# Second tile's scatter matrices: one wide comparison per step on VectorE, weights multiplied in by GpSimd and ScalarE, four one-hot slots, last expert row on VectorE

## The chip, the cores and the metric

The kernel runs on one core of a Trainium2 chip. The metric is the device time of one execution in microseconds (us). The core has five engines that run side by side, each with an instruction stream of its own, and meet at semaphores: TensorE (PE; PEld is its weight load), VectorE (DVE), ScalarE (ACT), GpSimd (POOL) and SyncE (SP), which here only starts transfers.

## What is computed

Two blocks follow each other on 256 tokens of width 2048. The first (gated MLP and stick-breaking attention) and the mixer of the second are not touched. The change lies in the product-key expert layer at the end, `peer_ffn`:

```python
# per token: 8 heads, 16 picks each = 128 picks out of 128 x 128 experts
s = einsum('thpc,hpnc->thpn', q, keys); sv, si = top_k(s, 16)
cand = sv[:, :, 0, :, None] + sv[:, :, 1, None, :]
cid  = si[:, :, 0, :, None] * 128 + si[:, :, 1, None, :]
top_s, top_j = top_k(cand, 16); eid = take(cid, top_j); gate = softmax(top_s)
act = gelu(einsum('thkd,td->thk', u[eid], x))        # 128 dot products per token
out = einsum('thk,thkd->td', gate * act, v[eid])     # 128 weighted rows per token
```

## The kernel before

The 256 tokens are two tiles of 128, one token per partition. For every pick r (128 a tile, 256 in all) GpSimd gathers one row of `u` per token into a ring of eight slots (line 614), and the dot product with the token's own vector is taken by one of two ways: slots 0, 1, 2, 4, 5 and 6 (`DVE_ROWS`) by a multiply-and-sum on VectorE (line 2076), slots 3 and 7 (`POOL_ROWS`) by a multiplication on GpSimd (line 622) and a sum on ScalarE (line 1323). After the last row of a tile ScalarE applies Gelu to its 128 dot products (line 1336) and VectorE multiplies them by the gates (line 2084): these are the weights.

The first 1440 columns of the output are not gathered. A dense weight matrix w (expert by token) is built and multiplied with all of `v`. Since an expert's number is 128 a + b, the 128 x 128 matrix of one token is the product of two one-hot matrices: `onehot_a` holds, per pick, a one (times the weight) at key a, `onehot_b` a one at key b. That is the scatter. To have picks on partitions, TensorE turns the two keys and the weights of a tile (line 1006, units `picks0` and `picks1`), and ScalarE copies the result to `picksT` (line 1104: row 0 holds a, row 1 b, row 2 the weights). Then there are 32 steps a tile, numbered m, of `SCATTER` = 4 tokens:

- VectorE: one comparison of 4 x 128 elements for `onehot_b` and four instructions of 128 elements that compare and multiply by the weight, for `onehot_a`. Tile 0 (`static_one_hots`, lines 2061 and 2065) is threaded between the dot products of tile 1, one step every three or four rows, and reads the row of numbers 0 to 127 from PSUM (`near_keys`). Tile 1 (`one_hots`, lines 2049 and 2053) stands behind the last dot product, in a hardware loop, and reads the numbers from SBUF (`iota_keys`).
- TensorE: four products into one of two PSUM places (line 1017). It waits for `onehot_done` and for the copy of two steps before (`w_stored`).
- ScalarE: copies the 512 columns to `wT` (line 1350, `store_one`).

There are two one-hot slots, so VectorE waits for the products of two steps before (`scattered`). After the last copy of tile 1 ScalarE rounds the first of `wT` (line 1366) and the stage that multiplies w with `v` begins: TensorE line 1037, with `v` streamed by SyncE (line 526), split by ScalarE (line 1375) and VectorE (line 2168), and the remaining 608 columns gathered by GpSimd (line 644) and added by VectorE (line 2150). The second slot of `v` and all gathers of line 644 but the first two wait until every scatter step is done, since they reuse the one-hot memory. The end of the program is the last layer norm and four stores.

Of the kernel before, what the change touches and what calls it, by code (L numbers as in the profile page):

```python
# [74 lines left out]
SCATTERS = P // SCATTER  # L75

# [11 lines left out]
EXPONENT, FINISH = 5, 8  # L88


def one_hot_row(m):
# [35 lines left out]
       ("picks0", B, False), ("picks1", A, False)]  # L127
# [35 lines left out]
def build(nc, x, norm_g, a_w_in, a_v_norm_g, a_w_s, a_b_s, a_w_out, b_w_in, b_w_out, final_g, ln_in_g_2, ln_in_b_2,  # L163
# [6 lines left out]
    with ctx:  # L170
# [158 lines left out]
        onehot_a = sb("onehot_a", [P, 2, SCATTER, N_KEYS], F32, SCR + 32 * KB)  # L329
        onehot_b = sb("onehot_b", [P, 2, SCATTER, N_KEYS], F32, SCR + 40 * KB)  # L330
# [98 lines left out]
        onehot_done = sem("onehot_done")  # L429
        scattered = sem("scattered")  # L430
# [113 lines left out]
        def _(pool):  # L544
# [82 lines left out]
            for j in range(TILES * BATCHES):  # L627
                s = 0
                for last in POOL_ROWS:
                    scale_row(j, last)  # L630
# [25 lines left out]
        def _(pe):  # L656
# [352 lines left out]
            def scatter(t):  # L1009

                with pe.Fori(0, P // SCATTER // 2) as i:
                    for s in range(2):
                        m = i * 2 + (t * (P // SCATTER) + s)
                        pe.wait_ge(onehot_done, m + 1)
                        pe.wait_ge(w_stored, m + 1)
                        for n in range(SCATTER):
                            last = mm(by_128[B][:, s * SCATTER + n, :], onehot_b[:, s, n, :], onehot_a[:, s, n, :],  # L1017
                                      start=True, stop=True)
                        last.then_inc(scattered, 1)
# [3 lines left out]
            for t in range(TILES):  # L1023
                pe.wait_ge(keys_known, t + 1)
                pe.wait_ge(wgt_done, t + 1)
                turn_picks(f"picks{t}", [pick_keys[:, t, half, :] for half in range(2)]
                           + [wgt[:, t * PICKS:(t + 1) * PICKS]])
                emptied(f"picks{t}")()
                scatter(t)
# [40 lines left out]
        def _(act):  # L1070
# [260 lines left out]
            def pick_gelu(t):  # L1331

                act.wait_ge(rows_used, (t + 1) * BATCHES * len(DVE_ROWS))
                act.wait_ge(rows_summed, (t + 1) * BATCHES * len(POOL_ROWS))
# [19 lines left out]
            def store_w(t):  # L1354

                with act.Fori(0, P // SCATTER // 2) as i:
                    for s in range(2):
                        store_one(t, i * 2 + s, s)
# [19 lines left out]
            for r in range(TILES * PICKS):  # L1378
# [7 lines left out]
                if s in POOL_ROWS:  # L1386
                    sum_row(j, s)
# [6 lines left out]
                for m in range(SCATTERS - 1):  # L1394
                    if r == one_hot_row(m) + 2:
                        store_one(0, m, m % 2)
            pick_gelu(1)
# [27 lines left out]
        def _(dve):  # L1425
# [620 lines left out]
            def one_hots(s, m, token):  # L2046

                dve.wait_ge(scattered, m + 1)
                v.tensor_tensor(onehot_b[:, s, :, :], iota_keys[:, :].unsqueeze(1).to_broadcast([P, SCATTER, N_KEYS]),
                                picksT[:, 1, bass.ds(token, SCATTER)].unsqueeze(2).to_broadcast([P, SCATTER, N_KEYS]),  # L2050
                                ALU.is_equal)
                for n in range(SCATTER):
# [188 lines left out]
```

## Time and profile before

| | us |
|---|---|
| median of 3 runs | 3037.32 |
| lowest and highest run | 3029.28 and 3040.89 |
| the profiled execution, its own time | 3035.28 |
| its span, first to last instruction | 3033.4 |

The profile is of one execution. Its times are counted from the first instruction; 1.9 us of the execution's time lie outside the span. The span has four parts here: dense products up to about 1780, the rows of `u` from there to 2437, the scatter of tile 1 from 2437 to 2495, and the product with `v` from there to 3011, with the last norm behind it. A line of the timeline gives start, duration, engine, line, operation, output and inputs, the count of instructions merged, and in brackets the idle time before it and who ended it.

### The profile page before, as it was taken

The numbers are of one execution on the slowest core, as the hardware profiler recorded it, in microseconds if no ns is written. First come the engines' busy times: TensorE is split into PE (matmuls) and PEld (weight loads), VectorE is DVE, ScalarE is ACT, GpSimd is POOL, SyncE is SP. The second block draws the span as 40 slices with busy tenths as digits, with TensorE's granted clock in tenths as the row PEclk, the third lists the DMA queues.
The fourth block names the chain that finished last, engine by engine and source line by source line (L and its number), as shares of the span: only waits on it lengthen the run. The fifth ranks groups of instructions, "written<-read, shape, count | busy, mean of one in ns | idle before, by whom it ended". The sixth has DMA issues, their size and how long they took to land.

```text
span 3033.4 us, 32464 instructions
## 1 busy us (share of the span) xinstructions
PE 2365.4 (78%) x10883; PEld 1981.4 (65%) x10883; DVE 2103.2 (69%) x2708; ACT 1228.6 (41%) x1293; POOL 830.6 (27%) x614
## 2 busy tenths in 40 slices
PE   8999999999999999899999950000122269999996
PEld 7888888888888888788888740000111158887885
DVE  5456455555444555745665679999998889898998
ACT  5444344444444554343444431212222234444443
POOL 1000000000000000000000048888877815555553
PEclk9999999999999999999999975555555589999998
DMA  8665556555666445555656469999999919999996
GB/s 282 203 185 185 179 179 189 185 193 184 188 187 188 146 163 195 157 169 163 183 185 223 160 254 411 421 417 418 408 411 410 419 49 347 338 346 351 343 344 236
DMA packets 183710, 772.91 MB, mean 255 GB/s; under 512 B 22236, under 2 KB 22288, under 8 KB 149680
## 3 DMA queue, kind: packets, MB, share of 16 engines
q1 hardware_dynamic: 123776, 409.00, 42.6%
q0 software_dynamic: 59824, 362.48, 29.5%
q8 instruction: 65, 1.06, 0.1%
q14 instruction: 45, 0.37, 0.0%
HBM read 769.29 MB, written 2.10 MB: 254 GB/s over the span
## 4 chain that ended last, share of the span: by engine, by line
PE 61%; DVE 19%; issue 8%; DMA 7%; POOL 3%; ACT 2%; DVEq 1%; POOLq 0%; SPq 0%; ACTq 0%
PE half L671 52%; DVE ring L2076 9%; PE half L1037 5%; DMA v_rows<-in_peer_v_rest,eid 3%; DMA ring<-in_peer_u,eid 2%; DMA v_raw<-in_peer_v_dense 2%; PE half L703 2%; POOL v_rows L644 2%; POOL ring L614 1%; DVE v_split L2168 1%; DVE onehot_a L2053 1%; DVE onehot_a L2065 1%; PE half L683 1%; DVE h L2150 1%; DVE v_odd L2150 0%
## 5 line engine op out<-in xcount | busy, mean ns | idle before, releaser
L671 PE MATMUL half<-w_split,xT 128*128 128x512 f32 x7008 | 1610.6, 391 | 8.0 <-DVE xT L1483 5.5
L671 PEld LDWEIGHTS half<-w_split,xT 128*128 128x128 f32 x7008 | 1314.3, 188 | 281.6 <-DVE xT L1483 7.0
L1436 DVE TENSOR_TENSOR w_split<-w_raw,w_split 128x1024 fp32r<-128x1024 f32 x592 | 722.3, 1225 | 740.8 <-ACT w_split L1082 739.8
L1082 ACT ACTIVATE w_split<-w_raw 128x1024 fp32r<-128x1024 f32 x592 | 626.2, 1059 | 910.1 <-PE half L671 875.1
L1037 PE MATMUL half<-v_split,w_x 128*128 128x512 f32 (+1 forms) x2304 | 507.4, 381 | 9.7 <-ACT v_split L1375 5.4
L1037 PEld LDWEIGHTS half<-v_split,w_x 128*128 128x128 f32 x2304 | 431.1, 188 | 85.8 <-issue 11.2
L2076 DVE CUSTOM_DVE_ANT_0 ring<-ring,half 128x2048 f32<-128x2048 f32 x192 | 434.1, 2284 | 47.5 <-DMA ring<-in_peer_u,eid 34.5
L644 POOL DMA_INDIRECT v_rows<-in_peer_v_rest,eid x256 | 280.7, 1097 | 286.6 <-issue 130.4
L1375 ACT ACTIVATE v_split<-v_raw 128x720 fp32r<-128x720 f32 x256 | 206.2, 807 | 273.2 <-DMA v_raw<-in_peer_v_dense 224.7
L614 POOL DMA_INDIRECT ring<-in_peer_u,eid x256 | 243.7, 952 | 259.2 <-DVE eid L2008 173.8
L1017 PE MATMUL half<-onehot_a,onehot_b 128*128 128x128 f32 x512 | 105.5, 371 | 256.9 <-DVE onehot_a L2065 240.3
L622 POOL TENSOR_TENSOR ring<-ring,h 128x2048 f32<-128x2048 f32 x64 | 289.4, 4522 | 41.9 <-DMA ring<-in_peer_u,eid 41.6
L548 POOL DMA_DIRECT2D row_a<-in_final_g x1 | 0.5, 537 | 1067.3 <-DVE ao L1698 1067.3
L1323 ACT ACTIVATE ring<-ring 128x2048 f32<-128x2048 f32 x64 | 122.2, 1910 | 412.1 <-POOL ring L622 412.1
L1017 PEld LDWEIGHTS half<-onehot_a,onehot_b 128*128 128x128 f32 x512 | 90.2, 266 | 272.5 <-DVE onehot_a L2065 249.8
L1006 PE MATMUL half<-ident,pick_keys 128*128 128x128 f32 x4 | 1.3, 434 | 341.1 <-DVE wgt L2084 332.4
L2168 DVE TENSOR_TENSOR v_split<-v_raw,v_split 128x720 fp32r<-128x720 f32 x256 | 230.7, 901 | 2.0 <-ACT v_split L1375 0.5
L1006 PEld LDWEIGHTS half<-ident,pick_keys 128*128 128x128 f32 x4 | 0.6, 204 | 341.6 <-issue 341.6
L2150 DVE SCALAR_TENSOR_TENSOR v_odd<-v_rows,wgt,v_odd 128x608 f32<-128x608 f32 x128 | 109.4, 855 | 36.2 <-DMA v_rows<-in_peer_v_rest,eid 32.6
L2150 DVE SCALAR_TENSOR_TENSOR h<-v_rows,wgt,h 128x608 f32<-128x608 f32 x128 | 108.9, 850 | 12.5 <-DMA v_rows<-in_peer_v_rest,eid 9.8
L548 POOL DMA_DIRECT2D row_a<-in_ln_g x1 | 0.5, 531 | 338.5 <-DVE xT L1483 338.5
L1350 ACT ACTIVATE wT<-half 128x512 f32<-128x512 f32 (+1 forms) x64 | 37.9, 592 | 84.9 <-PE half L1017 84.9
(312 smaller groups left out, 1206.0 us busy)
## 6 DMA issues: line engine op xcount, KB each, us to landing
w_raw<-in_a_w_in SPq DMA_DIRECT2D x192, 512.0 KB, 3.6
v_raw<-in_peer_v_dense SPq DMA_DIRECT2D x256, 360.0 KB
w_raw<-in_b_w_in SPq DMA_DIRECT2D x128, 512.0 KB, 3.5
w_raw<-in_w_in SPq DMA_DIRECT2D x112, 512.0 KB, 3.6
w_raw<-in_a_w_out SPq DMA_DIRECT2D x64, 512.0 KB, 4.3
w_raw<-in_b_w_out SPq DMA_DIRECT2D x32, 512.0 KB, 4.1
w_raw<-in_w_out SPq DMA_DIRECT2D x32, 512.0 KB, 4.8
w_raw<-in_peer_wq SPq DMA_DIRECT2D x32, 512.0 KB, 4.0
```

What stands on the lines that cost most here:

```text
L614: nc.gpsimd.indirect_dma_start(out=ring[:, s, :], out_offset=None, in_=peer_u_2[0], in_offset=bass.IndirectOffsetOnAxis(ap=eid[:, r:r + 1] ...
L622: nc.gpsimd.tensor_tensor(ring[:, s, :], ring[:, s, :], h[:, j // BATCHES, :], ALU.mult)\
L644: nc.gpsimd.indirect_dma_start(out=v_rows[r % V_SLOTS][:, :], out_offset=None, in_=peer_v_rest[0], in_offset=bass.IndirectOffsetOnAxis(ap= ...
L671: last = mm(ps[half][:, 2 * t + n, :], xt[:, xp, kk, tok], w_split[:, s, wp, n * BANK:(n + 1) * BANK], start=(k == 0 and xp == 0 and wp == ...
L1017: last = mm(by_128[B][:, s * SCATTER + n, :], onehot_b[:, s, n, :], onehot_a[:, s, n, :], start=True, stop=True)
L1037: ins = mm(flat[t][:, lo:lo + width], w_x[u][:, xp, 1 - t, s, :], v_split[s][:, vp, lo:lo + width], start=first and xp + vp == 0, stop=las ...
L1082: fn(w_split[:, k % SPLIT_SLOTS, 0, :], w_raw[:, k % RAW_SLOTS, :], ACT.Copy).then_inc(hi_done, 1)
L1375: fn(v_split[s][:, 0, cut], v_raw[s][:, cut], ACT.Copy).then_inc(v_hi, 1)
L1436: v.tensor_tensor(w_split[:, s, 1, :], w_raw[:, k % RAW_SLOTS, :], w_split[:, s, 0, :].bitcast(F32), ALU.subtract).then_inc(split_done, 1)
L2076: v.tensor_tensor_reduce(out=ring[:, s, :], in0=ring[:, s, :], in1=flat[1 - r // PICKS], scale=1.0, scalar=0.0, op0=ALU.mult, op1=ALU.add, ...
L2150: v.scalar_tensor_tensor(out=acc, in0=v_rows[m % V_SLOTS][:, :], scalar=wgt[:, bass.ds(i * BODY + m, 1)], in1=acc, op0=ALU.mult, op1=ALU.a ...
L2168: v.tensor_tensor(v_split[s][:, 1, cut], v_raw[s][:, cut], v_split[s][:, 0, cut].bitcast(F32), ALU.subtract).then_inc(v_lo, 1)
```

## The change

- `HOT_SLOTS` = 4: four one-hot slots, in one tensor `onehots` that holds a and b of a slot side by side. VectorE now waits for the products of four steps before, in both tiles.
- Tile 1's steps on VectorE (`plain_one_hots`) are one comparison of 2 x 4 x 128 elements each, without weights, against `near_keys[1]` in PSUM. The hardware loops over the steps on TensorE, ScalarE and VectorE become straight code.
- The weight is multiplied in afterwards, in place: GpSimd for three of the four tokens (`weigh_one_hots`, 384 elements a step, between its second and third gather of `v`), ScalarE for one (`weigh_one_hot`, `ACT_TOKENS` = 1). TensorE waits for both.
- The two keys of tile 1 are turned apart from the weights, as unit `keys1`, right behind the scatter of tile 0. `picks1` holds the weights alone.
- Row 255, the last one, is a row of VectorE (`by_pool`), not of GpSimd and ScalarE.
- On ScalarE the scaling of h (`weigh_h(1)`, line 1340) and the first rounding of v (`round_v(0, 0)`, line 1375) move from in front of the steps of tile 1 into steps 2 and 4, and the last copy of tile 0 and the copy of `keys1` stand before Gelu.

```diff
+HOT_SLOTS = 4
+ACT_TOKENS = 1
+LAST_ROW = TILES * PICKS - 1
+def by_pool(r):
+    return r % GATHER_SLOTS in POOL_ROWS and r != LAST_ROW
...
-        onehot_a = sb("onehot_a", [P, 2, SCATTER, N_KEYS], F32, SCR + 32 * KB)
-        onehot_b = sb("onehot_b", [P, 2, SCATTER, N_KEYS], F32, SCR + 40 * KB)
+        onehots = sb("onehots", [P, HOT_SLOTS, 2, SCATTER, N_KEYS], F32, SCR + 32 * KB)
+        onehot_a = [onehots[:, s, 0, :, :] for s in range(HOT_SLOTS)]
+        onehot_b = [onehots[:, s, 1, :, :] for s in range(HOT_SLOTS)]
...
+            def weigh_one_hots():
+
+                is_emptied(pool, "picks1")
+                for m in range(SCATTERS, TILES * SCATTERS):
+                    first, end = m * SCATTER + ACT_TOKENS, (m + 1) * SCATTER
+                    cut = onehot_a[m % HOT_SLOTS][:, ACT_TOKENS:, :]
+                    pool.wait_ge(onehot_done, m + 1)
+                    nc.gpsimd.tensor_tensor(
+                        cut, cut, picksT[:, 2, first:end].unsqueeze(2).to_broadcast([P, SCATTER - ACT_TOKENS, N_KEYS]),
+                        ALU.mult).then_inc(weighed_by_pool, 1)
...
                     if r == 2:
+                        weigh_one_hots()
                         pool.wait_ge(scattered, TOKENS // SCATTER + 2)
...
+                for m in range(t * SCATTERS, (t + 1) * SCATTERS):
+                    if t:
+                        pe.wait_ge(weighed_by_pool, m - SCATTERS + 1)
+                        pe.wait_ge(weighed_by_act, m - SCATTERS + 1)
+                    else:
                         pe.wait_ge(onehot_done, m + 1)
+                    pe.wait_ge(w_stored, m + 1)
+                    s = m % HOT_SLOTS
+                    for n in range(SCATTER):
+                        last = mm(by_128[B][:, m % 2 * SCATTER + n, :], onehot_b[s][:, n, :], onehot_a[s][:, n, :],
+                                  start=True, stop=True)
+                    last.then_inc(scattered, 1)
...
+            pe.wait_ge(keys_known, 2)
+            turn_picks("keys1", keys_in[1])
+            pe.wait_ge(wgt_done, 2)
+            turn_picks("picks1", [weights_in[1]])
+            scatter(1)
...
+            def weigh_one_hot(m):
+
+                act.wait_ge(onehot_done, m + 1)
+                for n in range(ACT_TOKENS):
+                    token = m * SCATTER + n
+                    cut = onehot_a[m % HOT_SLOTS][:, n, :]
+                    ins = fn(cut, cut, ACT.Copy, scale=picksT[:, 2, token:token + 1])
+                ins.then_inc(weighed_by_act, 1)
...
             pick_gelu(1)
-            store_one(0, SCATTERS - 1, (SCATTERS - 1) % 2)
-            picks_out("picks1", picksT[:, :, P:], 3)
-            weigh_h(1)
-            round_v(0, 0)
-            store_w(1)
+            picks_out("picks1", picksT[:, 2:3, P:], 1)
+            is_emptied(act, "picks1")
+            for m in range(SCATTERS + 2):
+                if m < SCATTERS:
+                    weigh_one_hot(SCATTERS + m)
+                if m >= 2:
+                    store_one(1, m - 2, m % 2)
+                if m == 2:
+                    weigh_h(1)
+                if m == 4:
+                    round_v(0, 0)
...
+            def plain_one_hots(m):
+
+                wide = [P, 2, SCATTER, N_KEYS]
+                token = m * SCATTER
+                dve.wait_ge(scattered, m - 1)
+                v.tensor_tensor(onehots[:, m % HOT_SLOTS, :, :, :],
+                                near_keys[1].unsqueeze(1).unsqueeze(1).to_broadcast(wide),
+                                picksT[:, 0:2, token:token + SCATTER].unsqueeze(3).to_broadcast(wide), ALU.is_equal)\
+                    .then_inc(onehot_done, 1)
...
             weights(1)
-            weights_turned(1)
+            is_emptied(dve, "keys1")
...
-            with dve.Fori(0, P // SCATTER // 2) as i:
-                for s in range(2):
-                    one_hots(s, i * 2 + (P // SCATTER + s), i * (2 * SCATTER) + (P + s * SCATTER))
+            for m in range(SCATTERS, TILES * SCATTERS):
+                plain_one_hots(m)
```

## Rows read from the trace of the kernel before

**Rows 1.** The page, parts 1 and 4: busy time; chain that ended last.

```profile
PE 2365.4 (78%) x10883; PEld 1981.4 (65%) x10883; DVE 2103.2 (69%) x2708; ACT 1228.6 (41%) x1293; POOL 830.6 (27%) x614
...
PE 61%; DVE 19%; issue 8%; DMA 7%; POOL 3%; ACT 2%; DVEq 1%; POOLq 0%; SPq 0%; ACTq 0%
```

**Rows 2.** Busy time by stretch: five engines, granted clock, DMA share, GB/s.

```profile
2300.00:2400.00 100.00, 22.82 (x88) 19.58 (x88) 84.77 (x114) 25.46 (x31) 82.96 (x50) 0.50 1.01 414
...
2441.00:2447.00 6.00, 5.40 (x23) 5.11 (x24) 5.33 (x17) 1.35 (x3) 0.00 (x0) 0.50 0.01 3
2447.00:2453.00 6.00, 4.03 (x31) 3.46 (x30) 5.53 (x18) 2.39 (x4) 0.00 (x0) 0.99 0.00 0
2453.00:2494.00 41.00, 29.28 (x206) 24.51 (x205) 40.16 (x125) 14.94 (x25) 0.00 (x0) 1.00 0.00 0
...
2600.00:2700.00 100.00, 99.71 (x458) 85.33 (x457) 91.76 (x115) 48.30 (x65) 55.50 (x52) 1.00 0.97 349
```

**Rows 3.** Timeline from the last rows of `u` to tile 1's first steps.

```profile
2426.93 2.07 PE L1017 MATMUL half<-onehot_a,onehot_b 128*128 128x128 f32 x8 [7.88 <-DVE onehot_a L2065]
...
2429.00 2.28 DVE L2076 CUSTOM_DVE_ANT_0 ring<-ring,half 128x2048 f32<-128x2048 f32 x1
2430.41 4.50 POOL L622 TENSOR_TENSOR ring<-ring,h 128x2048 f32<-128x2048 f32 x1 [5.40 <-DMA ring<-in_peer_u,eid]
2431.20 0.08 DVE L2076 DVE_READ_ACCUMULATOR2_ANT wgt<- 128x1 f32 x1
2434.94 1.91 ACT L1323 ACTIVATE ring<-ring 128x2048 f32<-128x2048 f32 x1 [6.38 <-POOL ring L622]
...
2437.03 0.31 ACT L1336 ACTIVATE wgt<-wgt 128x128 f32<-128x128 f32 x1
...
2437.38 0.29 DVE L2084 TENSOR_TENSOR wgt<-wgt,gate 128x128 f32<-128x128 f32 x1 [6.09 <-ACT wgt L1336]
...
2438.22 0.42 PE L1006 MATMUL half<-ident,wgt 128*128 128x128 f32 x1
2438.68 0.49 ACT L1104 ACTIVATE picksT<-half 128x384 f32<-128x384 f32 x1 [0.85 <-PE half L1006]
2439.07 0.70 ACT L1340 ACTIVATE h<-h 128x608 f32<-128x608 f32 x1
2439.59 0.69 DVE L2049 TENSOR_TENSOR onehot_b<-iota_keys,picksT 128x512 f32<-128x512 f32 x1 [1.93 <-ACT picksT L1104]
2439.67 1.49 ACT L1375 ACTIVATE v_split<-v_raw 128x720 fp32r<-128x720 f32 x2
...
2441.37 3.79 PE L1017 MATMUL half<-onehot_a,onehot_b 128*128 128x128 f32 x16 [2.72 <-DVE onehot_a L2053]
```

**Rows 4.** Timeline of the last steps of tile 1 and what follows.

```profile
2491.44 0.69 DVE L2049 TENSOR_TENSOR onehot_b<-iota_keys,picksT 128x512 f32<-128x512 f32 x1
...
2492.04 1.11 DVE L2053 TENSOR_SCALAR onehot_a<-iota_keys,picksT 128x128 f32<-128x128 f32 x4
...
2493.21 1.16 PE L1017 MATMUL half<-onehot_a,onehot_b 128*128 128x128 f32 x8 [0.47 <-DVE onehot_a L2053]
...
2494.51 0.60 ACT L1350 ACTIVATE wT<-half 128x512 f32 x1 [1.03 <-PE half L1017]
2495.14 0.63 ACT L1366 ACTIVATE w_x<-wT 128x512 fp32r<-128x512 f32 x1
```

**Rows 5.** Timeline of VectorE at 1754: 1024 elements, and what comes behind.

```profile
1754.09 1.22 DVE L1436 TENSOR_TENSOR w_split<-w_raw,w_split 128x1024 fp32r<-128x1024 f32 x1
1755.23 0.86 DVE L1950 MAX8 sv<-left 128x8 f32<-128x128 f32 x4
```

**Rows 6.** GpSimd's groups: shapes, count, busy us, mean ns, idle before.

```profile
L622 POOL TENSOR_TENSOR ring<-ring,h 128x2048 f32<-128x2048 f32 x64 | 289.4, 4522 | 41.9 <-DMA ring<-in_peer_u,eid 41.6
...
L558 POOL MEMSET ones<- 128x256 f32 x1 | 0.3, 312 | 0.1
...
L554 POOL MEMSET onward<- 128x128 f32 x1 | 0.2, 205 | 0.1
```

**Rows 7.** Line 2061, VectorE beside GpSimd: duration ns min/median/max, starts.

```profile
L2061 DVE TENSOR_TENSOR onehot_b<-half,picksT x32: 685/686/693, 2129.9 to 2425.2; 128x512 f32<-128x512 f32 x32
```

**Rows 8.** Timeline at 2054: a VectorE instruction with both inputs in SBUF.

```profile
2053.51 4.50 POOL L622 TENSOR_TENSOR ring<-ring,h 128x2048 f32<-128x2048 f32 x1 [1.48 <-DMA ring<-in_peer_u,eid]
...
2054.16 4.39 DVE L1979 TENSOR_TENSOR cand<-sv 128x512 f32<-128x512 f32 x1
```

More of the change, by code:

```diff
@@ L88 @@
 EXPONENT, FINISH = 5, 8
+LAST_ROW = TILES * PICKS - 1
+def by_pool(r):
+    return r % GATHER_SLOTS in POOL_ROWS and r != LAST_ROW
+DOTS = sum(not by_pool(r) for r in range(TILES * PICKS))
+SUMS = TILES * PICKS - DOTS
 def one_hot_row(m):
@@ L629, in _ @@
                 for last in POOL_ROWS:
-                    scale_row(j, last)
+                    if by_pool(j * GATHER_SLOTS + last):
+                        scale_row(j, last)
                     while s <= last:
@@ L1009, in scatter @@
             def scatter(t):
-                with pe.Fori(0, P // SCATTER // 2) as i:
-                    for s in range(2):
-                        m = i * 2 + (t * (P // SCATTER) + s)
-                        pe.wait_ge(onehot_done, m + 1)
[L1015 to L1019, printed above, removed]
+                for m in range(t * SCATTERS, (t + 1) * SCATTERS):
[3 more added lines that the diff above has]
+                    else:
+                        pe.wait_ge(onehot_done, m + 1)
+                    pe.wait_ge(w_stored, m + 1)
[4 more added lines that the diff above has]
+                    last.then_inc(scattered, 1)
             pe.sem_inc(scattered, 2)
             emptied("peer_q1")()
[L1023 to L1029, printed above, removed]
+            keys_in = [[pick_keys[:, t, half, :] for half in range(2)] for t in range(TILES)]
+            weights_in = [wgt[:, t * PICKS:(t + 1) * PICKS] for t in range(TILES)]
+            pe.wait_ge(keys_known, 1)
+            pe.wait_ge(wgt_done, 1)
+            turn_picks("picks0", keys_in[0] + [weights_in[0]])
+            emptied("picks0")()
+            scatter(0)
+            pe.wait_ge(keys_known, 2)
[3 more added lines that the diff above has]
+            scatter(1)
             def multiply_v(p, u, s, first=False, last=False):
@@ L1352, in store_one @@
                     .then_inc(w_stored, 1)
[L1354 to L1358, printed above, removed]
+            def weigh_one_hot(m):
[5 more added lines that the diff above has]
+                ins.then_inc(weighed_by_act, 1)
             act.sem_inc(w_stored, 2)
@@ L1393, in _ @@
                     fn(flat[A], h[:, 1, :], ACT.Copy).then_inc(h_copied, 1)
-                for m in range(SCATTERS - 1):
+                for m in range(SCATTERS):
                     if r == one_hot_row(m) + 2:
                         store_one(0, m, m % 2)
+                if r == one_hot_row(SCATTERS - 1) + 2:
+                    picks_out("keys1", picksT[:, 0:2, P:], 2)
             pick_gelu(1)
-            store_one(0, SCATTERS - 1, (SCATTERS - 1) % 2)
-            picks_out("picks1", picksT[:, :, P:], 3)
-            weigh_h(1)
-            round_v(0, 0)
-            store_w(1)
+            picks_out("picks1", picksT[:, 2:3, P:], 1)
[9 more added lines that the diff above has]
+                    round_v(0, 0)
             act.wait_ge(w_stored, TOKENS // SCATTER + 2)
@@ L2044, in bring_near @@
                 halving_by(near_half[t])
[L2046 to L2052, printed above, removed]
-                    ins = v.tensor_scalar(onehot_a[:, s, n, :], iota_keys[:, :], picksT[:, 0, bass.ds(token + n, 1)],
-                                          picksT[:, 2, bass.ds(token + n, 1)], ALU.is_equal, ALU.mult)
-                ins.then_inc(onehot_done, 1)
             def static_one_hots(m):
-                s, token = m % 2, m * SCATTER
-                dve.wait_ge(scattered, m + 1)
-                v.tensor_tensor(onehot_b[:, s, :, :], near_keys[1].unsqueeze(1).to_broadcast([P, SCATTER, N_KEYS]),
+                s, token = m % HOT_SLOTS, m * SCATTER
+                if m > 1:
+                    dve.wait_ge(scattered, m - 1)
+                v.tensor_tensor(onehot_b[s], near_keys[1].unsqueeze(1).to_broadcast([P, SCATTER, N_KEYS]),
                                 picksT[:, 1, token:token + SCATTER].unsqueeze(2).to_broadcast([P, SCATTER, N_KEYS]),
@@ L2064, in static_one_hots @@
                 for n in range(token, token + SCATTER):
-                    ins = v.scalar_tensor_tensor(out=onehot_a[:, s, n - token, :], in0=near_keys[1],
+                    ins = v.scalar_tensor_tensor(out=onehot_a[s][:, n - token, :], in0=near_keys[1],
                                                  scalar=picksT[:, 0, n:n + 1],
```

14 lines of the change are left out of this document (8 added, 6 removed).

## The prediction

> **What bounds the kernel now.** I read from the whole to the place. The page's busy shares and its chain name TensorE first and VectorE second [rows 1], but they average over stages. The table by stretch separates them [rows 2]. In the rows of `u` the transfers are full (DMA share 1.01 at 414 GB/s); in the product with `v` TensorE is busy 99.71 of 100 us. Between the two lies the scatter of tile 1, where transfers and GpSimd stand still and VectorE is busy 40.16 of 41.00 us, TensorE 29.28. So there VectorE sets the pace. The timeline of its last steps [rows 4] shows how: a comparison starts at 2491.44, the four instructions behind it at 2492.04, the next would start at 2493.07 (the products follow at 2493.21): 1.63 us a step, of which 0.60 is the comparison and 1.03 the other four. TensorE's products take 1.16, ScalarE's copy 0.60. The last product ends at 2493.21 + 1.16 = 2494.37, and the product with `v` hangs on it, by the copy at 2494.51 and the rounding at 2495.14. So whatever that end moves, everything behind moves too: behind it stands the same work, and no transfer of it but two pieces of v and two gathers runs ahead. The timeline of the hand-over [rows 3] gives the other piece: VectorE's last dot product ends at 2431.28, and then it waits 6.09 us, for row 255 on GpSimd (2430.41, 4.50 us) and ScalarE (2434.94, 1.91 us), before it may form the weights. The first comparison starts at 2439.59, the first product at 2441.37.
>
> **The change, part by part.**
>
> *Row 255 on VectorE.* It landed by 2430.41 (GpSimd was waiting for its transfer) and VectorE is free for it at 2431.2. The rows' dot product takes 2.28, 2.2 from start to start (2429.00 to 2431.20): done at 2433.5. Gelu then starts at 2433.6 in place of 2437.03, a gain of 3.4. Its cover is row 254: GpSimd's two first gathers of `v` are now issued some 10 us earlier, and 2 x 128 rows x 608 x 4 B = 0.62 MB would take 1.5 us at 414 GB/s if they went before row 255; 0.8 of that lies beside row 254, so 0.7 is the bound. They are issued after it, so I take 0.
>
> *Hand-over.* Gelu 0.31, the weights' multiplication 0.29, with the gap of 0.04 between: done at 2434.3. VectorE needs only the keys now; these were turned behind tile 0's scatter, whose products end at 2429.00, and copied before Gelu, which has 4 us of room. So the first wide comparison starts at 2434.3, not 2439.59. In parallel TensorE turns the weights (0.42 and a reaction, 2434.8) and ScalarE copies 128 columns (about the 0.31 of Gelu's 128): weights there at 2435.3, before the first comparison ends.
>
> *The wide comparison.* 1024 elements: the subtraction of that size takes 1.22, and the instruction behind it starts 1.14 after it [rows 5]; the 512 of now take 0.69 and 0.60, so both fit 0.53 us per 512 plus 0.07. I take 1.13 a step, against 1.63. The operand from PSUM costs nothing: 686 ns from PSUM [rows 7], 0.69 from SBUF.
>
> *GpSimd's multiplication,* 384 elements. Its multiplication of 2048 takes 4.52, and a memset takes 205 ns for 128 and 312 for 256 [rows 6], so about 0.1 is fixed: 0.1 + 384 x (4.42 / 2048) = 0.93, and 0.08 between two instructions: 1.01 a step. Low end: 384/2048 of 4.52 = 0.85. High end: 0.3 fixed (the whole of a small instruction's time) and 0.3 in between, 1.43 a step. I take 1.01, since the operation is the same and in place as well; no row shows its operand repeated along 128 elements. It lies beside VectorE's next comparison, and costs only its latency as long as it is under 1.13. GpSimd's queue has behind it only the gathers from the third on, and those waited for the whole scatter before as well.
>
> The GPSIMD Engine Reference of the Trainium skill, section Engine selection, speaks against this move: elementwise work on two inputs belongs on VectorE, GpSimd being about twice as slow. The rows agree (4.52 against 2.28 for 2048). It would count if GpSimd set the pace; by the 0.93 above it does not, so the sum stays as it is.
>
> *ScalarE:* one weighing (0.31) and one copy (0.60) a step, 0.91 in 1.13, and once 0.70 and 1.49 for the two moved jobs [rows 3]. Before, these two lay beside the first comparisons; now they are in the steps.
>
> *TensorE:* 1.16 for a step alone at the high clock [rows 4]. At the low clock 2.07 alone, and 3.79 for two steps back to back, so 1.71 for a further one [rows 3]; half of it, 0.86, at the high clock. The PSUM places bring 1.16 + 0.14 + 0.60 + 0.07 over two steps: 0.99 a step. Both are under 1.13 once the clock is up.
>
> **The sum.** First product: 2434.3 + 1.22 + 0.08 + 0.93 + 0.07 = 2436.6. The clock was granted at 0.50 until 2447 and in full from there, 5.6 us after the first product [rows 2, 3]; I take the same delay, 2442.3. By then TensorE starts four steps, at 2.07 and then 1.71 to 1.8 each, and the fourth ends at about 2444.0. ScalarE adds its 0.70 and 1.49 there, by which the weighing of the sixth step is done only at 2444.8 and its copy clears the way at 2445.4; its product ends at 2446.6. VectorE runs four steps ahead and is then held: the tenth comparison may start at 2446.7, where at its own pace it would at 2434.3 + 9 x 1.13 = 2444.5. So the start costs 2.2. From there 22 more at 1.13, and the last lasts 1.22: 2446.7 + 24.9 + 1.2 = 2472.8; weighing and reaction 1.0, products 0.07 + 1.16: 2475.0. The end of the scatter moves from 2494.4 to 2475.0, by 19.4: 5.3 from the earlier first comparison, 16 from 32 shorter steps, less 2.2 of start and less some 0.9 for the step's longer path at the end (wider comparison and weighing in series). The profiled execution took 3035.28, so 3015.9; the median of the runs lies 2.04 above it: 3037.3 - 19.4 = 3018.
>
> Costed at nothing: four slots in tile 0's scatter (VectorE waited nowhere for them that mattered; the transfers bound that stage [rows 2]); straight code for the loops (TensorE's streams elsewhere are straight and 99.71% busy); if the fetching of code did cost, it would by a few us, inside the range. The largest gain: no cost at the start, 21.6. The smallest of the forecast's kind: GpSimd at 1.43 a step, 2435.6 + 32 x 1.43 + 1.2 = 2482.6, a gain of 11.8.
>
> **The rivals.**
> - *GpSimd sets the pace.* For: its price is extrapolated, and a margin of 0.12 a step is thin. Against: fixed costs in rows 6 are small. At 1.4 a step the end is at 2481.6 and the time 3037.3 - 12.8 = 3025. At 1.80 a step nothing would be left.
> - *The clock stays low,* since TensorE has short products with waits between them. All 32 steps at 1.71: 2436.6 + 32 x 1.71 + 0.4 = 2491.7, a gain of 2.7, 3035. Against: with gaps of 0.47 in 1.63 us it rose before and stayed at 1.00 [rows 2, 4]; now they are shorter.
> - *VectorE and GpSimd shut each other out, and it gets slower.* Place: each wide comparison against each multiplication. That this exists is in the trace: an instruction of 512 elements with both inputs in SBUF took 4.39 us, not 0.69, and ended as GpSimd's multiplication did [rows 8]. A step would be 1.13 + 0.93 + 0.1 = 2.16, the end at 2434.3 + 32 x 2.16 + 1.2 = 2504.6, 10.2 later: 3047. It decides from 1.80 a step. Against: line 2061, with one input in PSUM as here, took 685 to 693 ns in all 32 instances beside a GpSimd 83% busy [rows 2, 7]. SBUF — State Buffer of the Trainium skill, section Who interferes with whom, says a VectorE instruction with at most one SBUF input doesn't contend with GpSimd; by that rule this rival falls, and the trace agrees with it (693 ns at most).
> - *The last row's move doesn't bring its 3.4,* if the transfer lands later. This costs at most that: 3021.
>
> **How the numbers follow.** The forecast with its neighbours, a gain of 15 to 22, gets 0.75 (the late row included); GpSimd's pace 0.15; the clock 0.05; the lock 0.05. The predicted time is 3018. The range reaches from the largest gain less the scatter of the runs, 3037.3 - 21.6 - 7 = 3009, to GpSimd at 1.43 with some of that scatter, 3037.3 - 11.8 + 3 = 3028. The bound of 0.5% is 15.2 us, about what a measurement of this kernel can tell from no change. The forecast lies 4 us beyond it, and the runs before differ by 11.6 among themselves, so 0.85 of its 0.75 count as faster and a third of GpSimd's case: 0.69. Slower by more than 0.5% needs 2.3 us a step: 0.03. The rest, 0.28, is within.
>
> **What would show it.** The first wide comparison at about 2434, taking 1.22 and followed by the next after 1.13 (right) or held by TensorE throughout (wrong). GpSimd's multiplication near 0.93 and waiting for VectorE each time; if VectorE waits for products and GpSimd is without gaps, the rival holds. Gelu about 0.1 behind row 255 on VectorE. The granted clock at 1.00 from 5 to 6 us after the first product. The last product near 2475, and the product with `v` as long as before (2495 to 3011). If that stage is longer, the gain was given back there, which I do not expect, since none of its inputs arrives otherwise than before.

## The result, and the profile after

The changed kernel takes 3017.51 us (median of 6 runs, 3014.29 to 3022.77) against 3038.43 for the kernel before (6 runs, 3029.28 to 3040.89): 20.9 us less, a ratio of 0.9938 with a 95% interval of 0.9926 to 0.9950. The forecast was 3018, with a range of 3009 to 3028. The profiled execution of after took 3014.29, its span is 3012.6. That the time lies within 0.5 us of the forecast is in part luck: the gain came out 1.5 larger than the 19.4 of the sum, and the kernel before 1.1 above the 3037.3 from which it was taken.

The hand-over and the first steps, in the timeline of the changed kernel (start, duration, engine, line, operation; in brackets the idle time before and who ended it), to be held against [rows 3]:

```profile
2429.50 2.28 DVE L2123 CUSTOM_DVE_ANT_0 ring<-ring,half 128x2048 f32<-128x2048 f32 x1
...
2431.71 2.28 DVE L2123 CUSTOM_DVE_ANT_0 ring<-ring,half 128x2048 f32<-128x2048 f32 x1
...
2434.03 0.31 ACT L1372 ACTIVATE wgt<-wgt 128x128 f32<-128x128 f32 x1 [2.10 <-DVE wgt L2123]
2434.37 0.29 DVE L2131 TENSOR_TENSOR wgt<-wgt,gate 128x128 f32<-128x128 f32 x1 [0.38 <-ACT wgt L1372]
2434.70 5.75 DVE L2113 TENSOR_TENSOR onehots<-half,picksT 128x1024 f32<-128x1024 f32 x5
...
2436.02 0.40 ACT L1396 ACTIVATE onehots<-onehots,picksT 128x128 f32<-128x128 f32 x1 [0.51 <-DVE onehots L2113]
2436.07 0.83 POOL L659 TENSOR_TENSOR onehots<-onehots,picksT 128x384 f32<-128x384 f32 x1 [8.17 <-DVE onehots L2113]
...
2440.77 4.62 DVE L2113 TENSOR_TENSOR onehots<-half,picksT 128x1024 f32<-128x1024 f32 x4 [0.33 <-PE half L1048]
...
2442.23 1.49 ACT L1414 ACTIVATE v_split<-v_raw 128x720 fp32r<-128x720 f32 x2
...
2444.63 7.64 PE L1048 MATMUL half<-onehots 128*128 128x128 f32 x61 [1.03 <-ACT wT L1386]
...
2445.80 6.88 DVE L2113 TENSOR_TENSOR onehots<-half,picksT 128x1024 f32<-128x1024 f32 x6 [0.41 <-PE half L1048]
```

Row 255 follows row 254 on VectorE (2431.71), the first wide comparison stands at 2434.70, and TensorE's first product came at 2436.95. VectorE is held by TensorE twice, for 0.33 and 0.41 us, and never again. (Held means that it waits for the products that free a slot.) Its comparisons then run without a gap, as VectorE's timeline shows when it is taken by itself:

```profile
2445.80 26.11 DVE L2113 TENSOR_TENSOR onehots<-half,picksT 128x1024 f32<-128x1024 f32 x23 [0.41 <-PE half L1048]
```

That is 23 comparisons in 26.11 us. One lasts 1.21 and the next starts 1.13 after it, so a comparison's last 0.08 lies beside the next one, and a hold costs its idle time and these 0.08. The last steps, to be held against [rows 4]:

```profile
2471.94 0.40 ACT L1396 ACTIVATE onehots<-onehots,picksT 128x128 f32<-128x128 f32 x1 [0.24 <-DVE onehots L2113]
2471.99 0.83 POOL L659 TENSOR_TENSOR onehots<-onehots,picksT 128x384 f32<-128x384 f32 x1 [0.30 <-DVE onehots L2113]
...
2472.94 0.97 PEld L1048 LDWEIGHTS half<-onehots 128*128 128x128 f32 x8 [0.16 <-POOL onehots L659]
...
2474.14 0.60 ACT L1386 ACTIVATE wT<-half 128x512 f32<-128x512 f32 x1 [0.53 <-PE half L1048]
2474.77 0.63 ACT L1405 ACTIVATE w_x<-wT 128x512 fp32r<-128x512 f32 x1
```

GpSimd waits 0.30 us a step for VectorE, TensorE 0.16 for GpSimd. By stretch (columns as in [rows 2]):

```profile
2453.00:2470.00 17.00, 16.97 (x123) 14.55 (x122) 17.00 (x16) 13.32 (x32) 12.45 (x16) 1.00 0.01 1
...
2580.00:2680.00 100.00, 100.00 (x461) 86.00 (x460) 92.47 (x117) 47.82 (x65) 56.84 (x52) 1.00 0.98 346
```

In the scatter TensorE is busy 16.97 of 17 us where it was 29.28 of 41, and ScalarE and GpSimd three quarters of the time, but VectorE still without a gap: it is still what sets the pace. TensorE's full share does not speak against it: its weight load waits 0.16 us a step for GpSimd, and behind 2445.80 VectorE is never held by it.

To compare traces I use one interval, which leaves out how long the rest took: from the start of row 254's dot product on VectorE to the first rounding of `wT` (L1366 before, L1405 after). It is 2495.14 - 2429.00 = 66.1 us before and 2474.77 - 2429.50 = 45.3 after, 20.9 less. In front of it the two traces differ by 0.5 us, behind it by as much the other way (538.3 and 537.8 to the end). So the whole gain lies in it, and nothing was given back.

### The profile page after: what moved, and what is told of

Read it like the earlier page. It is cut to its first block, busy times and chain, and to the rows that moved or that the text cites. A ratio compares the mean times of both kernels' runs of the same rounds, so it can differ in the third digit from the quotient of the medians.

```text
span 3012.6 us, 31949 instructions
## 1 busy us (share of the span) xinstructions
PE 2363.1 (78%) x10883; PEld 1980.9 (66%) x10883; DVE 2090.2 (69%) x2582; ACT 1236.3 (41%) x1324; POOL 849.3 (28%) x645
## 3 DMA queue, kind: packets, MB, share of 16 engines
q8 instruction: 69, 1.13, 0.2%
## 4 chain that ended last, share of the span: by engine, by line
PE 64%; DVE 18%; DMA 9%; issue 5%; POOL 2%; ACT 2%; DVEq 0%; SPq 0%; POOLq 0%; ACTq 0%
PE half L699 52%; DVE ring L2123 10%; PE half L1073 6%; DMA v_rows<-in_peer_v_rest,eid 4%; DMA v_raw<-in_peer_v_dense 2%; DMA ring<-in_peer_u,eid 2%; PE half L731 1%; POOL ring L629 1%; PE half L1048 1%; DVE v_split L2215 1%; DVE onehots L2102 1%; POOL v_rows L672 1%; PE half L711 1%; DVE v_odd L2197 0%; PE half L779 0%
## 5 line engine op out<-in xcount | busy, mean ns | idle before, releaser
L1048 PE MATMUL half<-onehots 128*128 128x128 f32 x512 | 102.5, 367 | 241.3 <-DVE onehots L2102 229.0
L1048 PEld LDWEIGHTS half<-onehots 128*128 128x128 f32 x512 | 89.4, 264 | 254.6 <-DVE onehots L2102 238.1
L1386 ACT ACTIVATE wT<-half 128x512 f32<-128x512 f32 x64 | 37.5, 586 | 53.9 <-PE half L1048 53.7
```

The lines of the kernel that those rows point to most:

```text
L1048: last = mm(by_128[B][:, m % 2 * SCATTER + n, :], onehot_b[s][:, n, :], onehot_a[s][:, n, :], start=True, stop=True)
```

## The experiments

Each edit is on the changed kernel unless it says otherwise. The interval, the first comparison and the holds of VectorE by TensorE come from the one trace of each run.

| run | interval | against after | first comparison behind row 254's start | time, us |
|---|---|---|---|---|
| before | 66.1 | +20.9 | 10.59 | 3038.43 |
| after | 45.3 | | 5.20 | 3017.51 |
| old_step | 60.2 | +15.0 | 6.09 | 3031.0 |
| two_slots | 64.2 | +18.9 | 5.21 | 3034.76 |
| three_slots | 47.2 | +2.0 | 5.20 | 3019.86 (one run) |
| keys_from_sbuf | 64.0 | +18.7 | 5.20 | 3036.76 |
| last_row_pool | 49.5 | +4.2 | 8.70 | 3017.76 (one run) |
| before_last_row | 62.3 | +17.0 | 7.09 | 3031.66 (one run) |
| keys_late | 47.2 | +2.0 | 6.44 | 3017.78 (one run) |
| jobs_early | 45.3 | +0.1 | 5.20 | 3016.4 (one run) |
| pool_four | 46.0 | +0.7 | 5.20 | 3017.45 (one run) |
| act_two | 45.7 | +0.5 | 5.20 | 3014.84 (one run) |
| prefill_two | 44.3 | -1.0 | 5.20 | 3016.04 |
| seven_eighths | 51.7 | +6.5 | 5.20 | 3020.98 |

A single time says little here, since the six of after spread over 8.5 us, and the kernel before, measured again beside these runs, had medians of 3037.53, 3034.96 (one run) and 3037.2; I read the interval first. The ratios below are to the kernel before as measured beside the run.

**old_step: what the step's own length carries.** All of the change but the wide step and its helpers.

```diff
-                plain_one_hots(m)
+                static_one_hots(m)        # one comparison of 512, four of 128 with the weight
...
-                        weigh_one_hots()
...
-                if m < SCATTERS:
-                    weigh_one_hot(SCATTERS + m)
```

> The changed kernel, but tile 1's steps on VectorE are the five narrow instructions of before, with the weight (reading the numbers from PSUM); GpSimd and ScalarE multiply nothing in; four slots, straight code, the early keys and row 255 on VectorE stay. My theory, that the length of VectorE's own step carries the gain: 1.63 us a step again, first comparison at about 2435.7 (it must wait for the weights now), last product ends near 2435.7 + 32 x 1.63 + 1.3 = 2489, 15 us later than in the changed kernel; time about 3032.5. Rival, that slots and straight code carry the gain by freeing VectorE of waits: the end stays within 5 us of 2474 and the time under 3023.

Ratio to before 0.9976 (0.9966 to 0.9986); 13.5 us slower than after, and 15.0 in the interval, as the theory had it. Two steps from its timeline of TensorE:

```profile
2472.36 1.16 PE L1043 MATMUL half<-onehots 128*128 128x128 f32 x8 [0.47 <-DVE onehots L2095]
2473.99 1.16 PE L1043 MATMUL half<-onehots 128*128 128x128 f32 x8 [0.47 <-DVE onehots L2095]
```

1.63 us a step again, with TensorE waiting 0.47 for VectorE, as in [rows 4]. VectorE was never held. So of the 20.9, 15.0 hang on the wide step with its helpers. Three pieces make them up: 14.5 between the first comparison and the last (2434.71 to 2485.24 here, 2434.70 to 2470.70 in after), 0.9 because the wide comparison does not wait for the weights (6.09 against 5.20), less 0.4 for the longer path behind the last comparison (3.61 here, 4.07 in after). The other 5.9 are hand-over, slots and straight code: 4.5 of these by the earlier first comparison (6.09 in place of 10.59), the other 1.4 between the first comparison and the last (51.85 in the kernel before, 50.53 here). There VectorE was held twice in the kernel before, for 0.67 and 0.47:

```profile
2443.61 0.69 DVE L2049 TENSOR_TENSOR onehot_b<-iota_keys,picksT 128x512 f32<-128x512 f32 x1 [0.67 <-PE half L1017]
...
2447.50 0.69 DVE L2049 TENSOR_TENSOR onehot_b<-iota_keys,picksT 128x512 f32<-128x512 f32 x1 [0.47 <-PE half L1017]
```

**two_slots and three_slots: whether the slots matter once weighing is a stage of its own.**

```diff
-HOT_SLOTS = 4
+HOT_SLOTS = 2                            # three_slots: 3
-                dve.wait_ge(scattered, m - 1)
+                dve.wait_ge(scattered, m + 1)   # three_slots: m
```

> The changed kernel with two one-hot slots in place of four. With weighing as a stage of its own between VectorE and TensorE, a slot is taken for 1.21 (comparison) + 0.07 + 0.83 (GpSimd) + 0.1 + 1.16 (products) + 0.1 = 3.4 to 3.5 us. Theory: with two slots a step then costs half of that, 1.7 to 1.75, the scatter ends 18 to 20 us later and the whole gain is gone: 3036 to 3038. Rival, that VectorE's 1.13 sets the pace whatever the slots: 3018.

> The changed kernel with three one-hot slots. A slot is taken for about 3.4 us, so three slots allow 1.13 to 1.17 a step, just what VectorE takes. Theory: within 1.5 us of four slots at the full clock, and more holding at the low clock (up to 3 us), so the scatter ends 1 to 4 us later. Rival, that the fourth slot is needed as much as the second pair: 6 us or more.

With two slots the ratio to before is 0.9998 (0.9986 to 1.0011): no gain can be told from the times, and of the interval's 20.9 us 2.0 are left, though each engine does exactly the same work. Its timeline shows VectorE in pairs, waiting for the products between them:

```profile
2469.40 2.52 DVE L2112 TENSOR_TENSOR onehots<-half,picksT 128x1024 f32<-128x1024 f32 x2 [0.94 <-PE half L1048]
...
2472.86 2.52 DVE L2112 TENSOR_TENSOR onehots<-half,picksT 128x1024 f32<-128x1024 f32 x2 [0.94 <-PE half L1048]
```

3.46 us for two steps, 1.73 each, as worked out. Not all of that is GpSimd's: the product waits for two ends that come together, GpSimd's multiplication (2471.53 in the trace) and ScalarE's copy of two steps before, which stands behind its weighing (2471.55). Three slots cost 2.0 us, within the 1 to 4 of the theory; VectorE is held three times there, by 0.88, 0.28 and 0.94, in the first ten steps. Behind them it shows no idle time, but its step is 1.15 (24 comparisons in 27.68 us) and not 1.13, and a third of 3.46 is 1.15: with three slots the slot still sets the pace by a hair, with four (0.87) it does not.

**keys_from_sbuf: the price of the lock that the place in PSUM avoids.**

```diff
-                                near_keys[1].unsqueeze(1).unsqueeze(1).to_broadcast(wide),
+                                iota_keys[:, :].unsqueeze(1).unsqueeze(1).to_broadcast(wide),
```

> The changed kernel, but the wide comparison reads the numbers 0 to 127 from SBUF (iota_keys) in place of PSUM (near_keys), so that it has two SBUF inputs while GpSimd multiplies. Theory (the third rival of the prediction, which the place in PSUM avoids): the two shut each other out, each step is 1.13 + 0.83 + about 0.1 = 2.06 to 2.2, and the scatter ends 29 to 34 us later, 3046 to 3052. Rival: no exclusion between these two operations, 3018.

The mechanism is there. The groups of VectorE and GpSimd in the stretch of the scatter (count, busy us, mean ns, idle before):

```profile
L659 POOL TENSOR_TENSOR onehots<-onehots,picksT 128x384 f32<-128x384 f32 x32 | 55.4, 1767 | 8.2 <-DVE onehots L2113 8.2
L2113 DVE TENSOR_TENSOR onehots<-iota_keys,picksT 128x1024 f32<-128x1024 f32 x32 | 55.3, 1804 | 0.0
```

The same two instructions took 0.827 and 1.210 us each in the changed kernel; here both last about 1.8, one waiting in the other's time, and no idle time shows it. It is not that reading SBUF is slower by itself: the first comparison, with no multiplication beside it yet, took 1.22 us, and the last multiplication, with no comparison beside it any more, 0.82. But its size was wrong, 18.7 in place of 29 to 34. Eight multiplications took 14.16 us, 1.77 a step, while 0.83 + 1.13 = 1.96: so some 0.2 of the two do overlap. What part of them that is, the runs leave open. The time is that of the kernel before, ratio 0.9998 (0.9988 to 1.0007); the interval is 2.2 shorter. This is also the other half of what the Trainium skill's SBUF — State Buffer states in the section Who interferes with whom, that a VectorE instruction with two SBUF inputs contends with a GpSimd instruction that reads SBUF; this run agrees, with 1.80 us for 1.21 on VectorE and 1.77 for 0.83 on GpSimd.

**last_row_pool and before_last_row: the last row undone, and alone.**

```diff
-LAST_ROW = TILES * PICKS - 1
+LAST_ROW = -1
```

and on the kernel before:

```diff
-                    scale_row(j, last)
+                    if j * GATHER_SLOTS + last != LAST_ROW:
+                        scale_row(j, last)
...
-                if s in DVE_ROWS:
+                if s in DVE_ROWS or r == LAST_ROW:
                     dve.wait_ge(row_landed[s], 16 * j + 16)
```

> The changed kernel with row 255 back on GpSimd and ScalarE. Theory: Gelu starts 3.0 us later (2437.0 in place of 2434.0, counted from the landing of row 255) and everything behind it with it: time up by 3. Rival, that a later start is taken up because VectorE has its comparisons ready in four slots: GpSimd then starts with four steps in hand and up to 3 x 0.13 a step is won back, time up by 1 or less.

> The kernel before with this part of the change alone: row 255 goes to VectorE. Theory: Gelu starts 3.5 us earlier against row 254, and since tile 1's steps begin only after the weights, the end of the scatter comes 3.5 us earlier too (66.1 us after the start of row 254 becomes 62.6, as putting it back cost 3.5 in the changed kernel's first comparison). Rival: the clock's time to rise varies by up to 2 us and hides part of it.

Undone, the first comparison comes 3.50 us later (8.70 for 5.20), and the end 4.2; alone on the kernel before, the first comparison comes 3.50 earlier and the end 3.9. So the row is worth 3.5. What is beyond that are holds of VectorE, 0.7 more of them in last_row_pool than in after (below) and one fewer in before_last_row than in the kernel before (0.67 alone). My rival for last_row_pool could not have come true: VectorE starts its comparisons behind the weights in either case, so it had none in hand.

**keys_late: the keys turned with the weights, as before.**

```diff
-            turn_picks("keys1", keys_in[1])
             pe.wait_ge(wgt_done, 2)
+            turn_picks("keys1", keys_in[1])
```

(and ScalarE's copy of them behind Gelu).

> The changed kernel, but the keys of tile 1 are turned and copied only after the weights are known, in front of the weights' own turn, as before the change. Theory: the first comparison comes 1.1 to 1.3 us later (turn of two 0.64, copy 0.38, reactions) and, as VectorE sets the pace, the end too. Rival: GpSimd and TensorE wait for the weights anyway, so nothing moves (under 0.3).

First comparison 1.24 later, as expected, the end 2.0 later.

**jobs_early: ScalarE's two jobs out of the steps.**

```diff
+                if r == LAST_ROW - 3:
+                    round_v(0, 0)
...
                     picks_out("keys1", picksT[:, 0:2, P:], 2)
+                    weigh_h(1)
...
-                if m == 2:
-                    weigh_h(1)
-                if m == 4:
-                    round_v(0, 0)
```

> The changed kernel, but ScalarE's scaling of h and first rounding of v are done while it waits for the last rows of u, not in steps 2 and 4. In the changed kernel TensorE stands for 1.03 us behind the rounding, and VectorE is held twice, 0.33 and 0.41. Theory: without them VectorE is held by 0.3 at most (the low clock's part), the scatter ends 0.4 to 0.7 earlier. Rival: it is all the low clock, no change.

The interval did not move (45.34 for 45.27; 0.4 to 0.7 less was expected), and read alone this says that the jobs cost nothing. But the clock differed. The granted clock rose 3.8 us behind the first product in after, and 5.5 to 5.9 behind it in jobs_early, keys_late and last_row_pool. The holds of VectorE, from the timelines:

| | clock up after | held |
|---|---|---|
| after | 3.8 | 0.33 + 0.41 = 0.74 |
| keys_late | 5.9 | 0.32 + 0.48 + 0.55 = 1.35 |
| last_row_pool | 5.5 | 0.32 + 0.48 + 0.58 = 1.38 |
| jobs_early | 5.7 | 0.32 + 0.48 = 0.80 |

Among the three with the late clock, the jobs account for the third hold, 0.55 to 0.58 us. The late clock costs 0.6 of holds with the jobs in place (1.35 to 1.38 against 0.74), and with the 0.08 of the third hold 0.7, which is just by how much the ends of keys_late and last_row_pool moved more than their starts. I take the jobs' 0.6 as supported, not shown: it rests on three single traces, and why the clock rose when it did stays open.

**pool_four and act_two: how near the helpers are to setting the pace.**

```diff
-ACT_TOKENS = 1
+ACT_TOKENS = 0                           # act_two: 2
```

> The changed kernel with GpSimd weighing all four tokens of a step (512 elements) and ScalarE none. It measures how near GpSimd is to setting the pace. In the changed kernel the multiplication takes 0.827 and stands 0.30 behind the one before. If those 0.30 are a wait for VectorE (my theory), GpSimd needs 4/3 x 0.83 = 1.10 and 0.08 between: 1.18 a step, the scatter ends 1 to 2 us later than in the changed kernel. If they are GpSimd's own gap (rival), a step is 1.40 and the scatter ends 7 to 8 us later.

> The changed kernel with ScalarE weighing two tokens a step and GpSimd two. ScalarE then has 2 x 0.31 to 0.40 and a copy of 0.58, 1.2 to 1.38 a step, over VectorE's 1.13. Theory: ScalarE sets the pace, the scatter ends 3 to 8 us later, GpSimd waits. Rival: its instructions overlap so far that it still keeps up, no change.

pool_four ended 0.7 later, less than the 1 to 2 expected: the multiplication of 512 takes 1.041, not 1.10, and fits into 1.13, with VectorE without a gap from 2446.60 on. The 0.30 were a wait. Of the 0.7 only 0.2 is the longer multiplication; VectorE was held three times at the start (0.48, 0.38 and 0.29, the clock rising 5.1 us behind the first product), which is 0.5 more than in after. In act_two the theory fell: two weighings, a copy, and the step stays at 1.13.

```profile
2463.35 0.69 ACT L1396 ACTIVATE onehots<-onehots,picksT 128x128 f32<-128x128 f32 x2
2463.39 0.61 POOL L659 TENSOR_TENSOR onehots<-onehots,picksT 128x256 f32<-128x256 f32 x1 [0.52 <-DVE onehots L2113]
...
2463.95 0.57 ACT L1386 ACTIVATE wT<-half 128x512 f32<-128x512 f32 x1
...
2464.48 0.69 ACT L1396 ACTIVATE onehots<-onehots,picksT 128x128 f32<-128x128 f32 x2
```

Two weighings of 0.40 each take 0.69 together, and the copy starts 0.60 behind the first: ScalarE's instructions overlap by some 0.1 each, so that durations summed (0.40 + 0.40 + 0.57 = 1.37) overstate what it needs. It shows no idle time in these steps, though, so it has hardly any room left. Of the 0.5 by which the interval is longer, 0.3 lie behind the last comparison.

**prefill_two: two comparisons in VectorE's idle time ahead of the last rows.**

```diff
+KEYS_AT = 26
+PREFILL = {SCATTERS: 247, SCATTERS + 1: 251}     # step: behind which row
...
+                for m, row in PREFILL.items():
+                    if r == row:
+                        is_emptied(dve, "keys1")
+                        plain_one_hots(m)
```

(TensorE turns the keys in front of step 26 of tile 0, and `jobs_early` is in it.)

> The changed kernel plus: tile 1's keys are turned behind step 25 of tile 0, VectorE does the comparisons of steps 32 and 33 while it waits for rows 248 and 252 (idle 1.60 us each there), and ScalarE's two jobs are early as in jobs_early. Theory: GpSimd can start as soon as the weights are there, the first product comes 0.5 to 0.9 us earlier, and VectorE has two comparisons fewer behind the weights; but TensorE at the low clock then holds it, so 1 to 2 us are gained: 3016. Rival, that VectorE's pace alone decides: the full 2.3 us, 3015.

Ratio to before 0.9932 (0.9917 to 0.9947), interval 1.0 us shorter than after's; the first product 6.97 behind row 254's start, not 7.45. The two comparisons cost nothing where they stand, but most of their 2.3 is lost again:

```profile
2413.96 1.22 DVE L2116 TENSOR_TENSOR onehots<-half,picksT 128x1024 f32<-128x1024 f32 x1
2415.65 2.29 DVE L2126 CUSTOM_DVE_ANT_0 ring<-ring,half 128x2048 f32<-128x2048 f32 x1 [0.47 <-DMA ring<-in_peer_u,eid]
...
2436.85 2.35 DVE L2116 TENSOR_TENSOR onehots<-half,picksT 128x1024 f32<-128x1024 f32 x2
2440.74 1.22 DVE L2116 TENSOR_TENSOR onehots<-half,picksT 128x1024 f32<-128x1024 f32 x1 [1.53 <-PE half L1053]
```

With its slots full, VectorE waits 1.53 and then 0.48 for TensorE. So of the theory the lower end came out. It is the best version here by its trace, but 3016.04 against 3017.51 is not a difference that these runs can tell.

**seven_eighths: VectorE's comparison an eighth shorter.**

```diff
+                    nc.gpsimd.tensor_scalar(onehot_a[m % HOT_SLOTS][:, 0, :], iota_keys[:, :],
+                                            keys_by_step[:, m - SCATTERS, 0:1],
+                                            picksT[:, 2, token:token + 1], ALU.is_equal, ALU.mult)
...
-                wide = [P, 2, SCATTER, N_KEYS]
+                wide = [P, 2 * SCATTER - 1, N_KEYS]
```

> The changed kernel plus: GpSimd builds one of the four onehot_a of a step by itself (comparison and weight in one instruction of 128 elements, from SBUF), so VectorE's comparison has 896 elements in place of 1024 (keys stored step by step for it), ScalarE weighs one token, GpSimd two; ScalarE's two jobs are early. If VectorE's own length sets the pace (theory), a step falls from 1.13 to 1.00 and the scatter ends 3 to 4 us earlier, 3014. GpSimd needs about 0.35 + 0.61 + 0.05 = 1.0 for it and could hold it at 1.05. Rival: the two PSUM places and ScalarE's copies already limit a step to 1.13, no gain.

It failed: 6.5 us more in the interval than after, 3020.98, ratio to before 0.9953 (0.9937 to 0.9969). GpSimd's groups in a stretch of the scatter, and VectorE's timeline:

```profile
L661 POOL TENSOR_SCALAR onehots<-iota_keys,keys_by_step,picksT 128x128 f32<-128x128 f32 x23 | 18.1, 788 | 0.0
L664 POOL TENSOR_TENSOR onehots<-onehots,picksT 128x256 f32<-128x256 f32 x23 | 14.0, 609 | 0.0
```

```profile
2459.56 1.09 DVE L2119 TENSOR_TENSOR onehots<-half,keys_by_step 128x896 f32<-128x896 f32 x1 [0.26 <-PE half L1053]
2460.92 1.09 DVE L2119 TENSOR_TENSOR onehots<-half,keys_by_step 128x896 f32<-128x896 f32 x1 [0.26 <-PE half L1053]
```

I had put the small instruction at 0.35, from its neighbours of 0.29 in the profile before; it took 0.788. Both GpSimd groups show no idle time, the step is 1.35 (2459.56 to 2460.92), and VectorE's 0.26 are put down to TensorE only because TensorE comes last in the row: the weight loads wait for GpSimd, so VectorE does too. That is the prediction's first rival in life: at 1.35 a step the interval is 6.5 longer, and 14.4 of its 20.9 remain. Whether 1.00 a step could be had otherwise stays open.

## Why the prediction was right

*What bounds.* Right. VectorE's length of a step set the pace and still does: old_step, which undoes the wide step and its helpers alone, gives back 15.0 of 20.9, and 14.5 of these lie between the first comparison and the last.

*Row 255 and the hand-over.* Right. First comparison at 5.3 behind row 254's start in the sum (2434.3), at 5.20 in the trace. The last row measured 3.5 both ways (predicted 3.4), the early keys 1.24. That the two gathers of `v` ahead of it cost nothing held: no idle time stands in front of row 255.

*The comparison.* 1.13 a step, as taken from [rows 5]; the duration was 1.21.

*GpSimd's multiplication.* On the safe side: 0.93 was taken, with a low end of 0.85, and it took 0.827. The three lengths that the runs have, 0.609, 0.827 and 1.041 for 256, 384 and 512 elements, make 1.69 ns an element and 0.18 fixed, against 2.2 ns an element in [rows 6]. So the fixed part had been put too low and the price of an element too high. That the operand repeated along the elements is what makes an element cheaper is likely, but no run here has a full operand at these lengths.

*ScalarE.* Sized 0.31 a weighing, measured 0.40; without effect, since its instructions overlap.

*The cost of the start* is the term that was mis-sized: 2.2 in the sum, 0.9 in the trace. The tenth comparison starts at 2445.80 where its own pace would bring it at 2434.70 + 9 x 1.13 = 2444.9; that is the 0.74 of holds and twice 0.08. The clock rose 3.8 us behind the first product, not the 5.6 of the kernel before, and by the other traces that is worth 0.7. The other 0.6 lie with ScalarE. Counted from row 254's start, the weighing of the sixth step, behind the rounding of `v`, was done at 14.5 (2444.0) and not at 15.8 as I had it; in last_row_pool, with the late clock, it was done at 15.25 once the 3.5 of the last row are taken off. With these 1.3 too much, 0.1 for the first comparison and 0.1 for GpSimd's shorter multiplication the difference between the predicted gain (19.4) and the measured (20.9) is accounted for.

*The split of the sum.* The times of the sum give 19.4, but the four terms named behind them, 5.3 + 16 - 2.2 - 0.9, make 18.2. Two of them are off. The 16 leaves out that VectorE was itself held in the kernel before, by 0.67 and 0.47 us, which the change takes away; and the longer path at the end is 0.5 by the sum's own times. Measured, the split is 5.4 for the earlier first comparison and 15.85 between the first comparison and the last (51.85 to 36.00), less 0.4 at the end.

*Straight code.* I had let the fetching of code cost a few us. No run prices it; that a step of old_step takes 1.63 with straight code, as it did in the loops, speaks for no cost.

*The rivals.* GpSimd's pace did not come true, with 0.30 of 1.13 to spare, but seven_eighths shows it to be real and its price as worked out: 1.4 a step was to leave 12.8 of the gain, 1.35 left 14.4. The clock staying low did not come true in any run. My argument against it was read loosely, though: with gaps of 0.47 it stayed up, but before it rose TensorE's only gap in the steps was 0.23, as the timeline of before shows:

```profile
2441.37 3.79 PE L1017 MATMUL half<-onehot_a,onehot_b 128*128 128x128 f32 x16 [2.72 <-DVE onehot_a L2053]
2445.38 2.85 PE L1017 MATMUL half<-onehot_a,onehot_b 128*128 128x128 f32 x16 [0.23 <-DVE onehot_a L2053]
```

The lock is real too, and is kept out by the place of the numbers in PSUM; it would not have made the kernel slower than before, as I had it, but just as fast: I had added both durations in full (2.16) and it took 1.77 a step, right beside the 1.80 at which nothing is left. (In [rows 8], too, the VectorE instruction ended 0.54 behind GpSimd's, at 2058.55 against 2058.01, and not with it.) What I did not put among the rivals is the slots: I costed them at nothing, looking at tile 0. For tile 1 they carry nearly everything, since with two of them 2.0 of the 20.9 are left. In the sum they were contained by letting VectorE run four steps ahead.

*The chances.* 0.69 for faster by over 0.5%: the ratio is 0.9938, and its interval up to 0.9950 just touches the bound, as near as the prediction had said.

## What to carry to other kernels

When one engine's step is cut in two and half of it handed to a neighbour, count for how long a buffer is now taken (here 3.46 us) and divide by the number of buffers: with two (1.73 a step) the longer path ate nearly all that the shorter step had won, with three (1.15) it was all but level with VectorE, with four it cost nothing. Work that is handed to GpSimd beside VectorE wants VectorE's inputs so placed that at most one is in SBUF, and the price of a GpSimd instruction should be measured for the very form that is used. A wait before a serial stage, here for the last row of a gather, is worth as much as the longest way through it: giving the last item to the faster engine brought 3.5 us alone.

## What the runs showed of the hardware that I had not expected

- GpSimd: a comparison and multiplication with two per-partition values over 128 elements of one input took 0.788 us, longer than a multiplication of 256 elements of two inputs (0.609). The GPSIMD Engine Reference of the Trainium skill, section Engine selection, has one-input operations at roughly line rate. For this form the run does not agree (VectorE's instructions of the same kind start 0.26 apart in [rows 4]), though one size does not part a fixed cost from a rate.
- GpSimd: multiplying by a value repeated along 128 elements cost 1.69 ns an element and 0.18 us fixed (256 to 512 elements), with two full operands of 2048 elements 2.2 ns an element in all.
- ScalarE: small instructions behind each other overlap by about 0.1 us each (two of 0.40 in 0.69).
- TensorE's granted clock rose 3.8 us behind the first product in after and 5.5 behind it in last_row_pool, whose scatter steps are the same code; over all fourteen traces it was 2.9 (two_slots) to 5.9 (old_step, keys_late). Between 3.8 and 5.9 it decides some 0.7 us of this stage.
- Mutual exclusion between VectorE and GpSimd shows as longer durations on both engines (1.80 and 1.77 for 1.21 and 0.83) and not as idle time.
